# First level of the scan's triangular inverse: from masked products on TensorE to masked neighbours laid in by transposes

## The reference

```python
def _wkv7_step(state, inp):
    r, w, k, v, a, b = inp
    sa = jnp.einsum('phvk,phk->phv', state, a)
    state = state * w[:, :, None, :] + sa[..., None] * b[:, :, None, :] + v[..., None] * k[:, :, None, :]
    return state, jnp.einsum('phvk,phk->phv', state, r)
...
    kk2 = _bidir(kk)
    _, out = lax.scan(_wkv7_step, state0, xs)      # 256 steps, 6 heads of 64, one scan in each direction
```

## Time and profile before

| | us |
|---|---|
| median of 3 runs | 1223.78 (1222.88 to 1224.12) |
| profiled execution | 1222.19 |
| its span | 1220.3 |
| PE busy | 1154.1 (95%) |
| DVE busy | 287.3 (24%) |
| ACT busy | 220.2 (18%) |
| GpSimd busy | 33.3 (3%) |

### The profile page before, as it was taken

The page is one execution under the profiler, slowest core; times in us unless marked ns, Lnnn a source line. Parts: engine busy times, 40 slices in busy tenths (PEclk is TensorE's granted clock), DMA queues, the critical chain, the costliest instruction groups (busy, mean ns, idle before and its releaser), DMA issues.

```text
span 1220.3 us, 14690 instructions
## 1 busy us (share of the span) xinstructions
PE 1154.1 (95%) x5893; PEld 503.9 (41%) x5893; DVE 287.3 (24%) x738; ACT 220.2 (18%) x452; POOL 33.3 (3%) x68
## 2 busy tenths in 40 slices
PE   7999999999999999999999999999999999999995
PEld 6875878754333333333333333333333333333331
DVE  1358656573111111111111111111111111111113
ACT  2244643511111111111111111111111111111112
POOL 1000112100000000000000000000000000000001
PEclk9999999999999999999999999999999999999998
DMA  9425002298999999979999999999999999999994
GB/s 332 161 63 198 2 1 75 78 399 330 397 429 428 429 428 428 429 307 428 430 429 429 428 428 430 428 429 429 429 429 428 429 430 428 429 429 429 428 427 173
DMA packets 41597, 429.66 MB, mean 352 GB/s; under 512 B 3756, under 2 KB 8851, under 8 KB 16739
## 3 DMA queue, kind: packets, MB, share of 16 engines
q1 hardware_dynamic: 39616, 426.10, 83.6%
q0 software_dynamic: 688, 2.06, 0.5%
q10 hardware_dynamic: 1267, 1.15, 0.4%
HBM read 428.24 MB, written 1.05 MB: 352 GB/s over the span
## 4 chain that ended last, share of the span: by engine, by line
PE 69%; DMA 21%; DVE 5%; ACT 3%; issue 1%; SPq 1%; ACTq 0%; POOL 0%; POOLq 0%; DVEq 0%
PE bank L1366 25%; DMA pool<-in_exp_w 20%; PE bank L1398 15%; PE bank L952 5%; PE bank L1340 3%; PE bank L962 3%; PE bank L1350 2%; PE bank L1250 2%; PE bank L1385 2%; DVE pool L1965 2%; DVE pool L1960 1%; PE bank L1120 1%; DVE pool L1962 1%; ACT pool L889 1%; PE bank L1136 1%
## 5 line engine op out<-in xcount | busy, mean ns | idle before, releaser
L1366 PE MATMUL bank<-pool 128*64 128x512 f32 x1024 | 230.9, 596 | 6.7 <-DMA pool<-in_exp_w 6.7
L1366 PE MATMUL bank<-ring,pool 128*64 128x512 f32 x1024 | 230.9, 596 | 4.9 <-DMA ring<-in_exp_w 4.9
L1398 PE MATMUL bank<-ring,pool 128*64 128x512 f32 x1024 | 226.8, 595 | 0.0
L1398 PEld LDWEIGHTS bank<-ring,pool 128*64 128x64 f32 x1024 | 70.7, 137 | 153.9 <-issue 153.9
L1366 PEld LDWEIGHTS bank<-pool 128*64 128x64 f32 x1024 | 70.3, 137 | 151.4 <-issue 138.8
L1366 PEld LDWEIGHTS bank<-ring,pool 128*64 128x64 f32 x1024 | 70.0, 137 | 149.8 <-issue 138.1
L1946 DVE TENSOR_SCALAR pool<-pool 128x128 f32<-128x128 f32 x64 | 19.4, 345 | 421.2 <-PE bank L1366 421.2
L1958 DVE TENSOR_SCALAR pool<-bank 128x512 f32<-128x512 f32 x32 | 22.2, 694 | 331.1 <-PE bank L1366 331.1
L1340 PE MATMUL bank<-pool 64*128 64x512 f32 x264 | 65.6, 614 | 0.7 <-ACT pool L893 0.7
L893 ACT ACTIVATE pool<-bank 128x512 f32<-128x512 f32 x32 | 19.1, 598 | 250.5 <-PE bank L1398 250.5
L1326 PE MATMUL bank<-pool 128*64 128x512 f32 x264 | 62.3, 592 | 1.0 <-DVE pool L1919 1.0
(11 more groups left out here) (301 smaller groups left out, 895.5 us busy)
## 6 DMA issues: line engine op xcount, KB each, us to landing
ring<-in_exp_w SPq DMA_DIRECT2D x127, 2048.0 KB, 20.5
pool<-in_exp_w SPq DMA_DIRECT2D x64, 2048.0 KB, 27.2
ring<-in_w_in SPq DMA_DIRECT2D x4, 2048.0 KB, 9.5
ring<-in_w_out SPq DMA_DIRECT2D x2, 2048.0 KB, 8.5
ring<-in_w_in SPq DMA_DIRECT2D x2, 1536.0 KB, 14.3
ring<-in_exp_w SPq DMA_DIRECT2D x2, 1024.0 KB, 23.6
ring<-in_w_in SPq DMA_DIRECT2D x1, 1632.0 KB, 6.9
pool<-in_consts SPq DMA_DIRECT2D x1, 1409.0 KB, 20.9
```

What stands on the lines that cost most here:

```text
L1366: last = mm(bank[4 + g][hp, :], lhs, w[:, k % 2, o:o + 512], start=False, stop=(k == KD - 1))
L1398: last = mm(bank[6][SLOTS * hf:SLOTS * hf + SLOTS, :], hT[:, k % 4, SLOTS * (k // 4):SLOTS * (k // 4) + SLOTS], w2s[k // 4][:, k % 4, 512 ...
```

## The change

Joining blocks of size 1 gives the identity plus the entry between two neighbours, so level 0 can be written down without a product: ym = I + mp where mp is masked to neighbours. The new constant C_X1 is this mask (one for each direction; it takes the place of C_T1). GpSimd multiplies and adds for direction 0 (two instructions of 128x512, in `early_columns` with n = 1, ahead of its copies). DVE does it for direction 1. s_x1m counts: 2pt+1 when GpSimd is done, 2pt+2 when DVE is. PE lays the four matrices of a direction into bank 4d+1 by transposes, as the start of the accumulation, and ACT evicts as before. The product, the identity matmul, the maskings and the update of level 0 are gone, and s_a and s_g count 12 for each pair where they counted 14. On PE, key_products(1) now follows key_products(0) and weigh, ahead of the new transposes. On DVE, the multiply and the add for direction 1 stand between the evictions of products and those of key products; between the two is a wait for s_x1m at 2pt+1.

```diff
-        c[:, C_T1 + d * P:C_T1 + d * P + P] = col == 2 * (row % HD) + d
+        c[:, C_X1 + d * P:C_X1 + d * P + P] = (row // 2 == col // 2) & (row % 2 == 1 - d) & (col % 2 == d)
...
+                def neighbours(d):
+
+                    pe.wait_ge(s_x1m, 2 * pt + d + 1)
+                    for j in range(4):
+                        last = mm(pview(4 * d + 1, 0, 4, P)[:, j], ym[:, d, j], ident, is_transpose=True, start=(j == 0),
+                                  stop=False, skip_group_check=True)
+                    last.then_inc(s_xn, 1)
+
...
                 key_products(0)
                 if pt:
                     weigh(2 * pt - 1)
-                for n in range(NL):
+                key_products(1)
+                for d in range(2):
+                    neighbours(d)
+                for n in range(1, NL):
                     for d in range(2):
-                        if n == 0:
-                            pe.wait_ge(s_prev, 4 * pt + 2 * d + 2)
-                            cross(0, d)
-                            mm(bank[4 * d + 1][:, :], ident, ident.unsqueeze(1).broadcast_to([P, 4, P]), start=True,
-                               stop=False, skip_group_check=True)
-                            continue
...
-                    if n == 0:
-                        key_products(1)
...
                 for d in range(2):
                     if n == 1:
                         pool.wait_ge(s_prev, 4 * pt + 2 * d + 2)
+                        if d == 0:
+                            mask, unit = (a.unsqueeze(1).broadcast_to([P, 4, P]) for a in (scan_const(C_X1, P), ident))
+                            step(nc.gpsimd.tensor_tensor(ym[:, 0], mp[:, 0, 1], mask, ALU.mult))
+                            nc.gpsimd.tensor_tensor(ym[:, 0], ym[:, 0], unit, ALU.add).then_inc(s_x1m, 1)
...
+                dve.wait_ge(s_prev, 4 * pt + 4)
+                link(V.tensor_tensor(ym[:, 1], mp[:, 1, 1], wide(scan_const(C_X1 + P, P), 4), ALU.mult))
+                dve.wait_ge(s_x1m, 2 * pt + 1)
+                V.tensor_tensor(ym[:, 1], ym[:, 1], wide(ident, 4), ALU.add).then_inc(s_x1m, 1)
                 key_products(0, 1)
-                masked(0, 0)
                 key_products(0, 0)
-                masked(1, 0)
                 key_products(1, 0)
                 key_products(1, 1)
```

More of the change, by code:

```diff
@@ L47 @@
 C_GM = C_MASK2 + 2 * 3 * P
-C_T1 = C_GM + NL * P
-C_HSEL = C_T1 + 2 * P
+C_X1 = C_GM + NL * P
+C_HSEL = C_X1 + 2 * P
 C_SELM = C_HSEL + 2
@@ L402, in encoder_kernel @@
         s_nqe = sem("key_products_evacuated")
+        s_x1m = sem("neighbour_terms_ready")
         s_xup = sem("inverse_evacuated")
@@ L1108, in key_products @@
                                 last.then_inc(s_nqf, 1)
+                def neighbours(d):
[4 more added lines that the diff above has]
+                    last.then_inc(s_xn, 1)
                 def cross(n, d):
-                    if n:
-                        pe.wait_ge(s_me, 12 * pt + 2 * n + d - 1)
+                    pe.wait_ge(s_me, 12 * pt + 2 * n + d - 1)
                     for jj in range(2):
[L1115 to L1120, removed]
+                        last = mm(pview(4 * d, 0, 2, P)[:, jj], m_early[(n - 1) % 4][:, d, jj],
+                                  y_late(d)[:, 2 * jj:2 * jj + 2], start=True, stop=True)
                     last.then_inc(s_a, 1)
@@ L1129, in update @@
                 def update(n, d):
-                    pe.wait_ge(s_g, 2 * NL * pt + 2 * n + d + 1)
-                    if n:
-                        pe.wait_ge(s_tev, 12 * pt + 2 * n + d - 1)
+                    pe.wait_ge(s_g, 12 * pt + 2 * n + d - 1)
+                    pe.wait_ge(s_tev, 12 * pt + 2 * n + d - 1)
                     for jj in range(2):
-                        lhs = tT[:, d, jj] if n else scan_const(C_T1 + P * d, P)
-                        last = mm(part(pview(4 * d + 1, 2 * P * jj, 2, P), n, 1 - d), lhs, gm[:, d, jj], start=False,
-                                  stop=(n == NL - 1), skip_group_check=True)
+                        last = mm(part(pview(4 * d + 1, 2 * P * jj, 2, P), n, 1 - d), tT[:, d, jj], gm[:, d, jj],
+                                  start=False, stop=(n == NL - 1), skip_group_check=True)
                     last.then_inc(s_xn, 1)
@@ L1453, in early_columns @@
                 if n > 4:
-                    pool.wait_ge(s_a, 2 * NL * pt + 2 * (n - 4) + 2)
+                    pool.wait_ge(s_a, 12 * pt + 2 * (n - 4))
                 elif n == 1 and pt:
-                    pool.wait_ge(s_a, 2 * NL * pt)
+                    pool.wait_ge(s_a, 12 * pt)
                 for d in range(2):
@@ L1459, in early_columns, with step @@
                         pool.wait_ge(s_prev, 4 * pt + 2 * d + 2)
+                        if d == 0:
+                            mask, unit = (a.unsqueeze(1).broadcast_to([P, 4, P]) for a in (scan_const(C_X1, P), ident))
+                            step(nc.gpsimd.tensor_tensor(ym[:, 0], mp[:, 0, 1], mask, ALU.mult))
+                            nc.gpsimd.tensor_tensor(ym[:, 0], ym[:, 0], unit, ALU.add).then_inc(s_x1m, 1)
                     nc.gpsimd.tensor_copy(half_cols(m_early[(n - 1) % 4][:, d], n), part(mp[:, d, 1], n, d)).then_inc(s_me, 1)
+            def step(ins):
+                psteps[0] += 1
+                ins.then_inc(s_pch, 1)
+                pool.wait_ge(s_pch, psteps[0])
             for pt in range(NP):
@@ L1742, in masked @@
                 def masked(d, n):
-                    dve.wait_ge(s_a, 2 * NL * pt + 2 * n + d + 1)
+                    dve.wait_ge(s_a, 12 * pt + 2 * n + d - 1)
                     V.tensor_tensor(gm[:, d], pview(4 * d, 0, 2, P), wide(gmask(n), 2), ALU.mult).then_inc(s_g, 1)
```

## The result

The changed kernel took 1227.05 us in the median (1225.97 to 1231.27, 8 runs) against 1223.89 us (8 runs) before: a ratio of 1.0033, 95% interval 1.0022 to 1.0045, or +4.0 us (the two medians lie 3.2 us apart, the means 4.2). The kernel became slower.

A forecast was written before the change was run, and what follows sets the result against it. PE, 95% busy, was taken to bound the kernel through an unbroken scan chain whose delay passes one to one to the end. Chain +2.3 and clock +2.5 gave +4.8 us, forecast median 1228.6 us, range 1224.6 to 1232.0.

The forecast's parts named there:

- case (a): Scan stage: the forecast itself, chain of 4.7 us and two or three clock falls, 1226.5 to 1231 us; chance 0.56.
- rival (b): Scan stage: PE's clock stays up, the chain alone costs +2.3 us, 1226.1 (+0.7 to +3.9); chance 0.22.
- L1105 starts: Scan, each pair: direction 1's key products on PE start 4.7 us after GpSimd's first instruction, 3.06 before in the first pair.
- distances, three pairs: Scan: longer waits from GpSimd's first instruction to L1105, +1.6 in the first pair, +0.3 in each other, +2.3 us.
- clock: Scan: PE's empty stretches let its granted clock fall two to three times, 1.1 us each, +2.5 us (nothing to 4.4).
- Rival (c): Level 0: GpSimd's two instructions cost only 0.72 us each, L1105 at 3.2, -2.3 us, 1221.5; chance 0.06.
- Rival (e): Scan stage: a distance of 5.25 us and three clock falls at full price, +8.3 us, 1232.1; chance 0.12.
- L1105 to ACT stays 1.8 us: Scan, direction 1: time from L1105's start to ACT's eviction unchanged, as transposes replacing updates cost nothing.
- the 2.3 counted on: Scan: number of clock falls expected over the three pairs, from two to three, at 1.1 us each.
- the full price: Clock: one fall costs 1.5 us where PE never waits, taken from the L1275 fills; 1.1 us estimated in the scan.
- rival (d): Expert stage: the scan's delay is hidden because DMA is full there, 1223.8 us; chance 0.04.
- upper bound of 8.1 us: Scan, PE: gain from 2.7 us of removed work in each of three pairs, if nothing else held L1105.

The follow-up runs named there:

- three fills: Changed kernel plus, per pair, three 128x512 matmuls nobody reads in PE's idle stretch ahead of direction 1's key products; ratio 1.0006 to the kernel before.
- no wait for GpSimd: Changed kernel with a separate semaphore for DVE's half, so DVE does not wait for GpSimd between multiply and add; ratio 1.0042 to the kernel before.
- second measurement: The changed kernel run again with nothing altered, on the same chip as the run with three fills; ratio 1.0051 to the kernel before.
- order alone: Kernel before, with only PE's key_products(1) moved to right behind weigh, ahead of level 0's cross products and identity fills; ratio 1.0011.

## Why the prediction was right

It forecast +4.8 us, and the measured +4.0 (2.7 to 5.5) lies within case (a), as does the median. The time alone does not single this case out: 1227.05 also lies in the range of rival (b), the chain without the clock (+0.7 to +3.9). What rules (b) out is the clock in the windows and the run with three fills. The steps against the profile after, in us after GpSimd's first instruction, first pair:

| step | forecast | measured |
|---|---|---|
| GpSimd's multiply ends | 1.33 | 1.26 |
| DVE's multiply, held by it, ends | 1.87 | 1.84 |
| GpSimd's add, held by DVE, ends | 3.00 | 2.96 |
| DVE's add, behind one copy, ends | 3.89 | 3.86 |
| L1105 starts | 4.7 | 4.52 |
| distances, three pairs | +2.3 | +1.7 |
| clock | +2.5 | +2.3 by the first measurement, +4.5 by the second (the ratio less 1.7) |

**The chain.** Right at each step, and 0.2 us too long at the end. DVE's eviction begins 0.08 us before its add has run out (123.17 against 122.45 + 0.80), and the sum adds two wake-ups of 0.1 behind DVE's add where only one follows it; the other, from GpSimd to DVE, passes under the copy. Three times 0.2 is the whole difference between 2.3 and 1.7. Without exclusion the distance would have been 4.2 us by the prediction's estimate; that the engines do exclude each other is shown by DVE's add of 1.63 us in the run with no wait for GpSimd. Rival (c) would have needed GpSimd's instructions at 0.72 us; they took 1.26. Rival (e) would have needed a distance of 5.25.

**The covering work.** "L1105 to ACT stays 1.8 us" held wherever the clock did (1.76 in the third pair and with three fills), so the exchange of updates for transposes cost nothing. GpSimd's eight copies, 3 us later, held nobody on PE: the profile names no wait for them.

**The clock.** The mechanism is shown by the run with three fills. Place and number were only half right, and that the term came out near its +2.5 is in part luck. Two of the four stretches at half clock stand right behind PE's idle time, the third pair has none there, and the other two lie inside the levels, where the forecast had none; against them the router's stretch of the earlier trace rows is missing in this execution.

From the mean clocks, 2 x (1 - clock) x time is the length at half speed: about 11.8 us a run before, 21.8 and 24.9 in the two measurements after, with three fills 12.0. A part of each lies behind PE's last work, where it costs nothing (7.6 us in the profile before, 5.0 in the one after). The difference of 10 to 13 us is three to four stretches of 3.4 us, more than the 2.3 counted on. What one costs is known only roughly: 0.85 us in the second pair and 1.1 in the first, as the forecast had it, but 5.1 us for the 12.9 us between the changed kernel and three fills, which is 1.35 us a stretch. In its second measurement the changed kernel's three longest runs and the other four lie 5.9 us apart for 13.7 us at half speed, 1.5 a stretch, which is the full price of the earlier trace rows.

The fills, which stand only ahead of L1105, bring the whole of the difference back. Single stretches inside the levels come without long idle time too (order alone, with 1.51 us at most in its first pair, has one at 176 to 180 and 6.8 us at 221 to 228). Why the idle time makes them more frequent was not settled.

**The end.** The expert stage passed the delay on, 928.9 us against 928.8; rival (d) is out. One reading of the earlier trace rows was loose, and nothing hangs on it: from 300 us on two slices of DMA lie under nine tenths, since the last of all reads 4.

**What the change was worth.** The 2.7 us of PE work that it takes from each pair were real. With DVE's evictions placed first, the same level 0 gives -3.5 us, under half of the upper bound of 8.1 us.

## What to carry to other kernels

When work is taken off the engine on the chain, look at what its next instruction waits for: here an eviction in another engine's queue, and what was put ahead of that eviction decided the sign of the change. In a queue, put what others need ahead of a wait. TensorE's idle time had a price of its own beyond its length here, since what followed could run at half clock; three matmuls a pair that nobody reads gave back most of the loss, and a better order gave back all of it and more.

## What the runs showed of the hardware that was not expected

- After 2.72 us of nothing on PE the clock fell in the second pair, in both profiles of the changed kernel, and after 2.78 and 2.79 us in the third it did not. After 2.24 us it fell in the first pair of the run that evicts between multiply and add; in the run with no wait for GpSimd it fell after 2.44 us (third pair) and not after 2.37 (second). Since stretches at half clock also came inside the levels, no one of these shows its cause by itself.
- The runs of one kernel lay 7 us apart, and time went with the clock: 1226 to 1233 us at mean clocks of 0.993 to 0.986.
- GpSimd's two-input instruction of 128x512 took 1.26 to 1.28 us when no DVE instruction with two SBUF inputs ran ahead of it, 1.59 to 1.63 when one did. The Trainium skill (GPSIMD Engine Reference, Elementwise — side-by-side cycle accounting) gives 4497 ns for 2048 elements; a quarter of that, as an estimate from the page, is 1.12 us, and the trace stands a little above it.
- Behind GpSimd's add its own next instruction, a copy, went first in every pair, and DVE's add took 0.80 us, where an eviction of the same width takes 0.62.
